# The PEER gate tiles of a hybrid encoder: one rounded 256-wide one-hot product per token, with the two halves added on VectorE, in groups of two tokens

## The reference, cut to what matters

```
s_top, i_top = top_k(sc, 16)                     # per token, head and half of the key
f_s, f_pos = top_k(all 16 x 16 sums, 16)          # the 16 best experts of each of 8 heads
gate = softmax(f_s)                               # 8 x 16 = 128 weights per token
a = einsum('td,tkd->tk', x, u_tab[eidx])
y = einsum('tk,tkd->td', gate * gelu(a), v_tab[eidx])
```

## Time and profile before

| what | value |
|---|---|
| median of 3 runs (lowest, highest) | 5016.57 us (5015.21, 5018.5) |
| profiled execution | 5020.93 us |
| its span, first to last instruction | 5018.9 us |
| mean granted TensorE clock | 0.989 of full speed |
| share of the span: PE, DVE, ACT, POOL | 97%, 64%, 22%, 56% |
| `stage_gates` in the trace | about 3010 to 3825 us |

### The profile page before, as it was taken

How to read it: one execution, slowest core, us unless ns; L and a number is a source line. 1 busy time by engine, 2 the same in 40 slices (tenths; PEclk the granted TensorE clock), 3 DMA queues, 4 the chain that set the end, 5 groups by cost and what they waited for, 6 DMA issues and landing times. The chain is left out here.

```text
span 5018.9 us, 87277 instructions
## 1 busy us (share of the span) xinstructions
PE 4885.3 (97%) x31904; PEld 4774.6 (95%) x31904; DVE 3202.4 (64%) x4749; ACT 1102.0 (22%) x1619; POOL 2831.5 (56%) x1682
## 2 busy tenths in 40 slices
PE   8999999999999999999999999999999999999998
PEld 8999999998998779999999999999999999999998
DVE  5777777773422434312067877787776888888865
ACT  4333333332323432101012111221121000000001
POOL 7100000004333325555577777888887999999986
PEclk9999999999999999999999999999999999999999
DMA  7333333334343535523243438999998888888852
GB/s 269 116 125 124 126 127 127 127 127 125 105 147 129 188 131 207 195 88 123 100 149 136 139 125 315 326 327 327 331 328 293 315 298 317 303 310 307 299 200 103
DMA packets 343033, 1010.54 MB, mean 201 GB/s; under 512 B 39712, under 2 KB 132096, under 8 KB 307216
## 3 DMA queue, kind: packets, MB, share of 16 engines
q1 hardware_dynamic: 165776, 526.23, 30.8%
q0 software_dynamic: 36864, 268.45, 14.1%
q10 hardware_dynamic: 140192, 213.34, 11.9%
HBM read 882.26 MB, written 126.76 MB: 201 GB/s over the span
## 5 line engine op out<-in xcount | busy, mean ns | idle before, releaser
L230 POOL TENSOR_SCALAR w_hi<-w_raw 128x1024 fp32r<-128x1024 f32 x694 | 770.3, 1110 | 1949.6 <-PE ps L764 982.2
L234 POOL TENSOR_TENSOR w_lo<-w_raw,w_hi 128x1024 fp32r<-128x1024 f32 x694 | 1716.5, 2473 | 130.3 <-POOL w_hi L230 128.3
L264 PE MATMUL ps<-h_hi,w_hi 128*128 128x416 f32 (+1 forms) x3808 | 1108.8, 329 | 34.7 <-POOL w_lo L234 17.3
L268 PE MATMUL ps<-h_hi,w_lo 128*128 128x416 f32 (+1 forms) x3808 | 1089.8, 324 | 0.0
L266 PE MATMUL ps<-h_lo,w_hi 128*128 128x416 f32 (+1 forms) x3808 | 1083.1, 322 | 0.0
L264 PE MATMUL ps<-ex_c_hi,w_hi 128*128 128x416 f32 x2048 | 718.1, 351 | 6.4 <-DVE ex_c_lo L2950 6.4
L268 PE MATMUL ps<-ex_c_hi,w_lo 128*128 128x416 f32 x2048 | 723.4, 353 | 0.0
L266 PE MATMUL ps<-ex_c_lo,w_hi 128*128 128x416 f32 x2048 | 715.4, 349 | 0.0
L264 PEld LDWEIGHTS ps<-h_hi,w_hi 128*128 128x128 f32 x3808 | 667.0, 190 | 46.6 <-issue 43.2
L266 PEld LDWEIGHTS ps<-h_lo,w_hi 128*128 128x128 f32 x3808 | 666.0, 189 | 6.0
L268 PEld LDWEIGHTS ps<-h_hi,w_lo 128*128 128x128 f32 x3808 | 663.4, 189 | 2.8
(11 more groups left out here) (333 smaller groups left out, 8233.6 us busy)
## 6 DMA issues: line engine op xcount, KB each, us to landing
w_raw<-weights SPq DMA_DIRECT2D x906, 512.0 KB
up<-up_out ACTq DMA_DIRECT2D x128, 208.0 KB
gate<-g_sb_g ACTq DMA_DIRECT2D x13, 2048.0 KB, 13.9
proj<-rows_out ACTq DMA_DIRECT2D x97, 272.0 KB, 2.1
sp_first<-up ACTq DMA_DIRECT2D x16, 832.0 KB, 6.6
ex_up<-up ACTq DMA_DIRECT2D x16, 832.0 KB
ex_gate<-gate ACTq DMA_DIRECT2D x16, 832.0 KB
sp_first<-proj ACTq DMA_DIRECT2D x48, 272.0 KB, 3.7
```

Source lines behind the costliest of these rows:

```text
L230: pool.tensor_scalar(self.whi[:, to, :], self.raw[:, slot, :], 1.0, 1.0, ALU.mult, ALU.mult).then_inc(self.hi_done, 1)
L234: pool.tensor_tensor(self.wlo[:, to, :], self.raw[:, slot, :], self.whi[:, to, :].bitcast(F32), ALU.subtract).then_inc(self.split_done, 1)
L264: pe.matmul(acc, hi, x, start=first, stop=False)
L268: mm = pe.matmul(acc, lo, x, start=False, stop=last)
```

## The change

A token's gate product is now one float32r matmul of 128 x 256. The stationary operand is the bare one-hot of the expert row (`rows`, no weight in it). The moving operand, `pairs`, holds the column's one-hot twice: once times the rounded weight `w_hi`, once times the rest `w_lo` of the weight. VectorE writes the bare one-hot once, and ScalarE makes both scaled copies of it, two activations per token. The product has two halves of 128 columns: ScalarE copies the first into `g` and the second into a buffer `rest`, and VectorE adds `rest` to `g` in place. A group is two tokens, so there are 208 groups instead of 104, and VectorE may be three groups ahead of the products instead of two. The store of a tile moves behind group 4 of the next one, for the last tile to the end of the stage. The load of `first_up` moves from the start of the stage to its end, since `rows` and `rest` lie in scratch memory at a fixed address. TensorE's loop body holds three tiles.

```
-    GROUP, BANKS = 4, 2
+    GROUP, DEPTH = 2, 3
-    DOTS_AFTER = [1, 1, 1, 2, 1, 1, 1, 2]
+    DOTS_AFTER = [1, 0, 1, 1, 0, 1, 1, 0] * 2
+    STORE_AT = 4
...
-                        mm = pe.matmul(ps[:, 4 + n % 2, t * N_KEYS:(t + 1) * N_KEYS], rows[:, n % 2, t, :],
-                                       cols[:, n % 2, t, :], start=True, stop=True)
+                        mm = pe.matmul(ps[:, 4 + n % 2, 2 * t * N_KEYS:2 * (t + 1) * N_KEYS], rows[:, at, t, :],
+                                       pairs[:, at, t, :, :].rearrange("s two c -> s (two c)"), start=True, stop=True)
...
+            def add_rest(group):
+                dve.wait_ge(copied, group + 1)
+                at = GROUP * (group % STEPS)
+                to = g[:, group // STEPS % 2, :, at:at + GROUP].rearrange("p c t -> p t c")
+                dve.tensor_tensor(to, to, rest[:, group % DEPTH, :, :], ALU.add).then_inc(rest_added, 1)
-            for group in range(TD // GROUP):
-                if needed(group - 1):
-                    dve.wait_ge(product, group - 1)
+            for group in range(GROUPS):
+                if needed(group - DEPTH + 1):
+                    dve.wait_ge(product, group - DEPTH + 1)
                 for t in range(GROUP):
...
-                    dve.tensor_scalar(rows[:, group % 2, t, :], iota, of(0), of(2), ALU.is_equal, ALU.mult)
-                    ins = dve.tensor_scalar(cols[:, group % 2, t, :], iota, of(1), None, ALU.is_equal)
+                    dve.tensor_scalar(rows[:, group % DEPTH, t, :], iota, of(0), None, ALU.is_equal)
+                    ins = dve.tensor_scalar(pairs[:, group % DEPTH, t, 0, :], iota, of(1), None, ALU.is_equal)
                 ins.then_inc(hot, 1)
...
+                if group >= DEPTH:
+                    add_rest(group - DEPTH)
...
+            def scale(group):
+                act.wait_ge(hot, group + 1)
...
+                for t in range(GROUP):
+                    token = GROUP * group + t
+                    one_hot = pairs[:, group % DEPTH, t, 0, :]
+                    act.activation(pairs[:, group % DEPTH, t, 1, :], one_hot.bitcast(F32), ACT.Copy,
+                                   scale=w_lo[:, token:token + 1])
+                    i = act.activation(one_hot, one_hot.bitcast(F32), ACT.Copy, scale=w_hi[:, token:token + 1])
+                i.then_inc(scaled, 1)
+            def store(q):
+                act.wait_ge(rest_added, added_by + STEPS * (q + 1) + 1)
+                act.dma_start(io["gate"][q], g[:, q % 2, :, :]).then_inc(stored[q % 2], 16)
...
+            store(G_TILES - 1)
+            act.dma_start(sparse.first_up[:, :, :], io["up"].rearrange("b p t -> p b t")[:, 0:VSET, :]
+                          ).then_inc(sparse.first_up_loaded, 16)
```

More of the change, by code:

```diff
@@ L2703, in _, with tile @@
             mm.then_inc(sparse.x_ready, 1)
-            def tile(q):
+            def tile(q, turn):
                 def up_pieces(n):
@@ L2713, in tile @@
                         up_pieces(0)
-                    pe.wait_ge(hot, group + 1)
+                    pe.wait_ge(scaled, group + (scaled_by + 1))
                     if needed(group - 1):
@@ L2723, in tile, with three @@
                         up_pieces(n)
-            rounds(pe, G_TILES, tile)
+            tile(0, 0)
+            def three(q):
+                for turn in range(1, 1 + DEPTH):
+                    tile(DEPTH * q + turn, turn)
+            rounds(pe, (G_TILES - 1) // DEPTH, three)
         @block.vector
@@ L2741, in _ @@
                         s += 1
+            for group in range(GROUPS - DEPTH, GROUPS):
+                add_rest(group)
             while s < SLOTS:
@@ L2748, in _ @@
             act.activation(ident_r[:, :], core.ident, ACT.Copy).then_inc(ident_ready, 1)
-            act.dma_start(sparse.first_up[:, :, :], io["up"].rearrange("b p t -> p b t")[:, 0:VSET, :]
-                          ).then_inc(sparse.first_up_loaded, 16)
+            act.activation(w_hi.bitcast(F32R), w_lo, ACT.Copy).then_inc(ident_ready, 1)
+            def scale(group):
+                act.wait_ge(hot, group + 1)
+                if group == 0:
+                    act.wait_ge(rest_added, added_by + 1)
+                for t in range(GROUP):
[8 more added lines that the diff above has]
+                act.dma_start(io["gate"][q], g[:, q % 2, :, :]).then_inc(stored[q % 2], 16)
+                act.activation(sparse.first_gate[:, q, :].rearrange("p (c t) -> p c t", t=G_TILE),
+                               g[:, q % 2, 0:VSET, :], ACT.Copy).then_inc(sparse.first_gate_copied, 1)
+            scale(0)
+            scale(1)
             for q in range(G_TILES):
@@ L2757, in _ @@
                     act.wait_ge(product, group + 1)
+                    if needed(group - DEPTH + 1):
+                        act.wait_ge(rest_added, added_by + group - DEPTH + 2)
                     at = GROUP * n
-                    act.activation(g[:, parity, :, at:at + GROUP].rearrange("p c t -> p t c"),
-                                   ps[:, 4 + n % 2, :].rearrange("p (t c) -> p t c", t=GROUP), ACT.Copy
-                                   ).then_inc(copied, 1)
-                    if n == STEPS - 1:
-                        act.wait_ge(copied, STEPS * (q + 1))
-                        act.dma_start(io["gate"][q], g[:, parity, :, :]).then_inc(stored[parity], 16)
-                        act.activation(sparse.first_gate[:, q, :].rearrange("p (c t) -> p c t", t=G_TILE),
-                                       g[:, parity, 0:VSET, :], ACT.Copy).then_inc(sparse.first_gate_copied, 1)
+                    halves = ps[:, 4 + n % 2, :].rearrange("p (t two c) -> p t two c", t=GROUP, two=2)
+                    act.activation(g[:, parity, :, at:at + GROUP].rearrange("p c t -> p t c"), halves[:, :, 0, :],
+                                   ACT.Copy)
+                    act.activation(rest[:, group % DEPTH, :, :], halves[:, :, 1, :], ACT.Copy).then_inc(copied, 1)
+                    if group + 2 < GROUPS:
+                        scale(group + 2)
+                    if q and n == STORE_AT:
+                        store(q - 1)
                     for p in UP_AFTER[n]:
```

16 lines of the change are left out of this document (14 added, 2 removed).

## The result

The changed kernel takes 5162.65 us (median of 4 runs, 5157.04 to 5167.4) where the kernel before takes 5016.79 beside it: a ratio of 1.0288, with a 95% interval from 1.0276 to 1.0300. It is slower by 146 us, and the prediction of 5005 us (4974 to 5042) missed it altogether. The span of the profiled execution is 5158.8 us.

What follows compares the result with a forecast made beforehand. It took TensorE to bound the kernel, with VectorE becoming the bound by a little after the change: 5020.93 - 51 + 31 + 9 = 5010 us profiled, 5005 us as the median, range 4974 to 5042.

Steps and rivals of the forecast that it cites:

- What bounds the kernel: Gate stage: TensorE, busy 600.00 of 600 us, sets the pace at 61.5 us a tile; time saved there comes back in full.
- Both have slack: VectorE, busy 48.6 us of each 61.5 us tile, and GpSimd, 52.1, have room, though near its end.
- TensorE's term: Gate products: one rounded 256-column matmul per token saves 3.9 us a tile, 51 us in 13 tiles; floor 57.6 us.
- ScalarE's term: Copies, scalings, Gelus and issues in the gate stage take 46 of 57.6 us a tile, so they fit.
- VectorE's term: Gate stage: cheaper `rows` one-hots, sixteen additions at 0.45 us and more holding; tile taken as 60.0 us, giving back 31 us.
- The upper price of 0.58: VectorE's strided additions on `g`: up to 0.58 us each; tile then about 62.5 us, 64 us given back.
- The holding: VectorE's time held by GpSimd: 12.2 us for 14.4 us holdable work before, 16.9 for 20.0 after, +4.7 us a tile.
- The rival (b): Gate stage: VectorE and GpSimd saturate, scalings and gathers come late; 63 us a tile, 5045 us (5027 to 5065), chance 0.25.
- The Trainium skill's line penalty: Additions on `g`: each access leaving a 16-byte line pays a penalty, putting additions at their upper price.
- The ends of the stage: Start counted as nothing; at the end, the late load of `first_up` costs 8 to 9 us, bounds 5 and 14.

Runs made afterwards that it cites:

- e1: Kernel before with rows and columns in the rounded type, one single-pass 128-wide product per token, rest of the weight left out: 5020.74 us, ratio 1.0009.
- e4: Changed kernel with VectorE's additions left out, so the gates lack the product with the rest of the weight: 5027.09 us, ratio 1.0020.
- the table of four: Stage times by products and maker of columns' one-hots: fp32/VectorE (kernel before) 817.7 us, fp32/ScalarE (e5) 811.1, rounded/VectorE (e1) 815.0, rounded/ScalarE (e6) 767.4.
- e6: Kernel before with rounded one-pass 128-wide products (rest of the weight left out) and the columns' one-hots made by ScalarE: 4968.15 us, ratio 0.9902.
- e5: Kernel before with the columns' one-hots made by ScalarE instead of VectorE, four-pass products kept: 5010.97 us, ratio 0.9987.
- e12: e8 with half of the first up blocks loaded at the stage's start, half ahead of the last gate store, two `rest` buffers: 4993.1 us, ratio 0.9949.
- e9: Changed kernel with every dot reading the first gathered buffer and the other gathers no longer waiting for dots: 5118.81 us, ratio 1.0202.
- e10: e7 with every dot reading the first gathered buffer and the other gathers no longer waiting for dots: 5111.57 us, ratio 1.0188.
- e7: Changed kernel with additions reading the product's second half from PSUM, ScalarE's copy into `rest` dropped, additions two groups behind instead of three: 5155.18 us, ratio 1.0272.
- e8: Changed kernel with columns' one-hots on ScalarE, one product half copied by ScalarE into contiguous rows, the other read by VectorE from PSUM: 4989.89 us, ratio 0.9942.
- e11: Changed kernel with each gather issued one step later in GpSimd's order: 5133.06 us, ratio 1.0230.

## Why the prediction was wrong, point by point

**What bounds the kernel.** Wrong, and the main step that failed. In the terms of the sum, TensorE's -51 us came as -2.7 (`e1`), VectorE's +31 as +136.5 (the changed kernel against `e4`), and the +9 of the end as 8.9 us of waiting. "Both have slack": VectorE's 12.9 us of idle time in each tile of 61.5 were not slack. A gather is issued by GpSimd, in one queue with splits that wait for TensorE; so in a stage that TensorE paces, VectorE waits for gathers. Let TensorE ask for more and the gathers come earlier, but the splits then fall on one-hots for the whole of the time that VectorE had spent partly held and partly idle (112 + 126 us before, 237 in `e1`). That this room doesn't exist is shown by `e1` and by the table of four. That a page of the profile shows TensorE at 600.00 of 600 us did not make it the only bound.

**TensorE's term**, 51 us: near in size only where VectorE has room. The rounded products (128 columns wide in `e6`, expected at 45 to 55 us) brought 43.7 us between `e5` and `e6`, and 2.7 us between the kernel before and `e1`.

**ScalarE's term**: it fits, as said. Scalings follow each other 0.29 us apart, its stretch is half full (299 of 600), and where TensorE waits for scalings, ScalarE had waited for VectorE's one-hots. The whole remainder beside the additions is 8 us (`e4` against `e1`), the end of the stage included.

**VectorE's term**: the plain `rows` one-hot saved its 0.05 us. The additions cost 0.58 us in the median and not 0.45, 27 us more in 208 of them. The upper price of 0.58 that the prediction gave them was met by luck: it rests on a cycle of 0.96 ns that no row shows. The rows give 1.04 ns an element (416 in 0.50 us, 2048 in 2.20), and 0.34 us with ScalarE's surcharge in full, 256 x 1.08 ns, is 0.62. The holding was sized by a rate, 0.84 us for each microsecond of holdable work, and that rate belongs to a VectorE that stands idle while splits run. Better is the share that VectorE's own work gets once it is the bound. In the 600 us of `e1`, 237 are lost, which leaves 0.605. The changed kernel's tile holds 32 x 0.40 + 10 x 2.20 + 16 x 0.58 = 44.1 us of work; over the share read in `e1` that is 73 us a tile, and gate stores at 3113.86 and 3907.46, eleven tiles apart, make it 72.1. The same reckoning without additions, 34.8 / 0.605 = 57.5, is too low for `e4`, whose gate stores make it 61.7 a tile; I take it that where TensorE and VectorE tie, each also waits for the other, which no run took apart. So the share, read after the result, serves only where VectorE is well past the tie. In the sum, 9.3 us of additions became 136.5 / 13 = 10.5 us a tile.

**The rival (b)** had the right mechanism, the pair of VectorE and GpSimd saturated with gathers waiting in the same queue. Its price was wrong: 63 us a tile where 72 came, since it started from the same false room. It stood at 0.25.

**The Trainium skill's line penalty**, "SBUF — State Buffer", section "Door 1: The DMA port swizzle", spoke for dear additions. The measured 0.58 us for 256 strided elements agrees, against 0.50 us for 416 contiguous ones (3831.37 to 3831.87 in the kernel before), and is the upper price that I had derived from ScalarE's copy. By the rule alone the forecast should have leaned to (b).

**The ends of the stage.** The time was right: 8.9 us more of TensorE's waiting. The reason was half of it: I put it on the load of `first_up`, and VectorE did wait for it last (9.61 us). But `e12` shows that with this load early most of the wait only moves. The last gate store now stands behind the last product, a Gelu, two copies and an addition, and SyncE and GpSimd wait for its landing (issued 3956.84, SyncE goes on at 3964.10); before, it was issued at 3817.05, 7.7 us ahead of TensorE's last matmul.

**What stays open.** About 45 us go with the loop of dots and gathers (`e9`, `e10`). Part of them may be TensorE's clock: over the same 600 us it was granted 0.93 in the changed kernel and 0.98 in `e9`, whose 416-column matmuls took 38 us less in the stage, and the two were not separated. The rest behaves like a split meeting whatever stands there, but I tried no kernel without splits, and in the two cut kernels the dots no longer wait for gathers either, so the loop was cut on both sides at once. What the 8.0 us between `e4` and `e1` consist of was not taken apart.

## What to carry to other kernels

Before a wait is counted as room, follow its releaser: if it ends at the engine that is to be relieved, through a queue that also holds up this one, it is not room. The quick test is the relief alone, without its price, as in `e1`; and where two engines tie, only a change that relieves both shows anything. When VectorE shares its stage with GpSimd's elementwise work, budget it by the share of time that its own work gets when it is full (here 0.6, read in `e1`; it gives too short a time for `e4`, near the tie), and move holdable operations to ScalarE first.

## What the runs showed of the hardware

- After a VectorE addition of 128x256 with strided output and first operand (every 32nd fp32 element) the next operation starts 0.58 us later in the median, with its other operand in SBUF (changed kernel, 178 unheld ones) as with it in PSUM (`e7`, 189). Where it lies changes the holding, not the price.
- GpSimd is held as well, where the addition starts first. In the changed kernel 60 gathers were issued while an addition with two SBUF operands was running: they took 1.40 us in the median. The 65 others took 1.03, also where an addition started during them (3193.27, the addition at 3193.72, itself unheld at 0.68 us). In `e7`, 63 gathers issued during an addition that reads PSUM took 1.03 too.
- ScalarE makes a one-hot of 128x128 in two operations of 0.29 us each to the next start (`e8`: two of them from 3401.58 to 3402.17), and a Gelu among them left the same 0.55 us of idle time behind it (3405.26) as in the changed kernel (3405.22).
- The granted clock was 0.93 over the 600 us in which TensorE of the changed kernel was busy 525, a mean of its two levels (1.2 and 2.4 GHz), and its first group of 416-column matmuls took 369 ns each instead of 358. In `e11`, busy 527, it was granted 0.98.
